# Expert stage: gate by tanh, rows stored already modulated, all low parts of the weights on VectorE

## The reference, cut to what matters

```python
x = x + ga1 * y                                   # y = hybrid_mixer(...)
h = rmsnorm(x, g_norm_ffn) * (1.0 + sc2) + sh2    # sh2, sc2, ga2 from silu(c) @ w_ada + b_ada
aff = softmax(h @ w_router)                       # 2048 x 16
g, idx = top_k(aff.T, 256)                        # per expert
xs = h[idx]                                       # 16 x 256 x 1024
a, u = xs @ w_gate, xs @ w_up                     # 16 x 256 x 768
out = rmsnorm(x + ga2 * scatter_add(idx, (silu(a) * u) @ w_down * g), g_final)
```

## Time and profile before

| what | value |
|---|---|
| median of 3 runs | 3539.58 us (3536.52 to 3541.98) |
| span of the profiled execution (its own time beyond the span isn't given) | 3526.4 us |
| PE, PEld busy | 3097.0 us (88%), 2192.4 us (62%) |
| DVE, ACT, POOL busy | 2266.7 (64%), 1427.3 (40%), 992.7 (28%) |
| mean granted TensorE clock | 0.934 |

### The profile page before, as it was taken

The page is one execution under the profiler, slowest core; times in us unless marked ns, Lnnn a source line. Parts: engine busy times, 40 slices in busy tenths (PEclk is TensorE's granted clock), DMA queues, the critical chain, the costliest instruction groups (busy, mean ns, idle before and its releaser), DMA issues. The chain is left out here.

```text
span 3526.4 us, 44830 instructions
## 1 busy us (share of the span) xinstructions
PE 3097.0 (88%) x14689; PEld 2192.4 (62%) x14689; DVE 2266.7 (64%) x2823; ACT 1427.3 (40%) x2136; POOL 992.7 (28%) x514
## 2 busy tenths in 40 slices
PE   6899999999786999999999988971988989899892
PEld 1455555555785556556555647850888878888782
DVE  1133333333675777777777764557888989889893
ACT  0133333332223566666556644330334343333433
POOL 0000001100453332332333212211445444444441
PEclk9999999999776999999999999985999999999996
DMA  8412111121322011011001004341565666656656
GB/s 320 149 59 69 59 59 64 66 67 48 102 89 58 4 31 31 5 31 31 23 13 29 5 20 157 125 141 57 156 203 169 191 186 181 196 165 195 190 145 226
DMA packets 252530, 362.92 MB, mean 103 GB/s; under 512 B 34356, under 2 KB 168503, under 8 KB 250808
## 3 DMA queue, kind: packets, MB, share of 16 engines
q1 hardware_dynamic: 243128, 326.91, 28.5%
q0 software_dynamic: 9216, 33.56, 4.3%
HBM read 278.60 MB, written 81.83 MB: 102 GB/s over the span
## 5 line engine op out<-in xcount | busy, mean ns | idle before, releaser
L465 PE MATMUL bank<-w_in_sb,h_T 128*128 128x512 f32 (+1 forms) x1440 | 610.2, 579 | 2.1 <-DVE h_T L614 2.1
L1614 PE MATMUL ebank<-gathered_T,w_gate_up 128*128 128x256 f32 x4608 | 564.9, 284 | 20.5 <-ACT w_gate_up L1656 12.7
L1614 PEld LDWEIGHTS ebank<-gathered_T,w_gate_up 128*128 128x128 f32 x4608 | 560.2, 190 | 24.4 <-issue 23.5
L1075 PE MATMUL abank<-scores,head_v 128*128 128x512 f32 x1152 | 546.0, 602 | 2.2 <-ACT scores L1113 2.2
L1038 PE MATMUL abank<-head_qT,head_kT 96*128 96x512 f32 x1728 | 504.6, 437 | 22.9 <-POOL head_qT L1017 22.9
L465 PEld LDWEIGHTS bank<-w_in_sb,h_T 128*128 128x128 f32 x1440 | 271.1, 191 | 298.9 <-issue 298.7
L1038 PEld LDWEIGHTS abank<-head_qT,head_kT 96*128 96x128 f32 x1728 | 327.7, 190 | 169.9 <-issue 94.7
L1024 POOL TENSOR_TENSOR scores<-scores,max_for_pool 128x1536 f32<-128x1536 f32 x64 | 221.1, 3476 | 570.9 <-ACT max_for_pool L1107 570.9
L1101 ACT ACTIVATE scores<-abank 128x512 f32<-128x512 f32 x576 | 314.2, 608 | 77.0 <-PE abank L1038 71.2
L1075 PEld LDWEIGHTS abank<-scores,head_v 128*128 128x128 f32 x1152 | 218.6, 194 | 180.3 <-issue 162.8
L1628 PE MATMUL ebank<-w_down,hidden_T 128*128 128x512 f32 x1152 | 303.0, 418 | 21.0 <-POOL w_down L1545 20.8
(11 more groups left out here) (261 smaller groups left out, 4138.3 us busy)
## 6 DMA issues: line engine op xcount, KB each, us to landing
w_gate_up_whole<-in_w_exp_gate SPq DMA_DIRECT2D x48, 1024.0 KB, 5.9
w_gate_up_whole<-in_w_exp_up SPq DMA_DIRECT2D x48, 1024.0 KB, 9.0
w_down_whole<-in_w_exp_down SPq DMA_DIRECT2D x192, 256.0 KB, 2.9
ada_w<-in_w_ada SPq DMA_DIRECT2D x12, 2048.0 KB, 12.8
scratch_ret<-ret_rows SPq DMA_DIRECT2D x72, 256.0 KB, 2.5
x_tile<-in_x_all SPq DMA_DIRECT2D x18, 512.0 KB
w_in_sb<-in_w_in SPq DMA_DIRECT2D x4, 2048.0 KB, 15.0
chunk_qk<-scratch_ret SPq DMA_DIRECT2D x16, 512.0 KB
```

Of the source, the lines that this page charges most:

```text
L465: m = pe.matmul(banks[bank][:, 0:n], hT[u][:, k, :], w_in[:, k, lo:lo + n], start=(k == 0), stop=(k == KD - 1))
L1075: m = pe.matmul(banks[5 + j % 2][:, :], v1[u][:, kt, :], sc[j % 2][:, kt, :], start=(kt == 0), stop=(kt == T - 1))
L1614: x = pe.matmul(banks[f % 3][:, j * CAP:(j + 1) * CAP], w_gu[c][:, wp, j, k, o:o + P], xsT[:, xp, k, :], start=(k == 0 and n == 0), stop=( ...
```

## The change

Four edits go together. (1) In mix_out the modulation is done on rows ahead of the transposes: x2 is multiplied by its statistic and the scale row, then the shift row is added, and the transposed halves are only copied from PSUM. The rows stored for the gather are so already modulated, and the expert stage has no modulate step; ACT rounds straight from the PSUM bank and DVE subtracts from it. (2) The two rows come from the columns: SP stores columns 24 to 39 to DRAM at the end of modulation, and mix_out loads them broadcast to all partitions. (3) The gate is x (1 + tanh(x / 2)) / 2. (4) DVE makes all low parts of the weights; POOL only issues its indirect DMAs.

```diff
@@ -226,6 +226,8 @@
+            sp.wait_ge(s_fold, 5)
+            sp.dma_start(scratch["ffn_rows"].rearrange("o (j p) -> p (o j)", p=P), perm["modcols"][:, 0, 24:40], allow_slow_non_contiguous=True).then_inc(perm["ffn_rows_stored"], 16)
@@ -1202,6 +1204,8 @@
+        xs = sb("x2_scaled", [P, D])
+        ffn_rows = sb("ffn_rows", [P, 2, D])
@@ -1241,6 +1245,8 @@
+            sp.wait_ge(perm["ffn_rows_stored"], 16)
+            sp.dma_start(ffn_rows[:, :, :].rearrange("p j d -> p (j d)"), scratch["ffn_rows"].partition_broadcast(P)).then_inc(r_loaded, 16)
@@ -1292,7 +1298,7 @@
             def router(m):
...
-                pe.wait_ge(r_loaded, 16)
+                pe.wait_ge(r_loaded, 32)
@@ -1353,12 +1359,9 @@
             def router(m):
...
-                    o = h2T[:, 4 * g:4 * g + 4, :]
...
-                    dve.tensor_tensor(o, banks[4 + g][:, :].rearrange("p (k n) -> p k n", k=4), last(perm["modcols"][:, 0, 32 + 4 * g:36 + 4 * g], P), ALU.mult).then_inc(sg["h2T"].sem, 1)
-                    sg["h2T"].wait(dve, m, 2 * g + 1)
-                    dve.tensor_tensor(o, o, last(perm["modcols"][:, 0, 24 + 4 * g:28 + 4 * g], P), ALU.add).then_inc(sg["h2T"].sem, 1)
+                    dve.tensor_copy(h2T[:, 4 * g:4 * g + 4, :].rearrange("p k n -> p (k n)"), banks[4 + g][:, :]).then_inc(sg["h2T"].sem, 1)
@@ -1389,7 +1392,12 @@
-                dve.tensor_scalar(xn[:, :], x2[u][:, :], st[:, 1:2], None, ALU.mult).then_inc(sg["x2_normed"].sem, 1)
+                if first:
+                    dve.wait_ge(r_loaded, 32)
+                dve.scalar_tensor_tensor(xs[:, :], x2[u][:, :], st[:, 1:2], ffn_rows[:, 1, :], ALU.mult, ALU.mult).then_inc(sg["x2_scaled"].sem, 1)
+                sg["x2_scaled"].wait(dve, m)
+                settled(dve)
+                dve.tensor_tensor(xn[:, :], xs[:, :], ffn_rows[:, 0, :], ALU.add).then_inc(sg["x2_normed"].sem, 1)
@@ -1535,24 +1542,9 @@
-            def rest_up(e, c):
-                sg["gu_rounded"].wait(pool, e, 2 * c + 2)
-                pool.tensor_tensor(w_gu[c][:, 1, 1], w_gu_whole[c][:, 1, 1], w_gu[c][:, 0, 1].bitcast(F32), ALU.subtract).then_inc(sg["up_rest"].sem, 1)
-            def rest_down(e, i):
-                sg["d_rounded"].wait(pool, e, i + 1)
-                x = w_d[i % RING]
-                pool.tensor_tensor(x[:, 1, :], w_d_whole[i % RING][:, 1, :], x[:, 0, :].bitcast(F32), ALU.subtract).then_inc(sg["d_rest_late"].sem, 1)
             def turn(e, u, ahead):
-                rest_up(e, 2)
...
-                    rest_up(e + 1, 0)
-                for i in range(RING, ND):
-                    rest_down(e, i)
-                if ahead:
-                    rest_up(e + 1, 1)
@@ -1594,7 +1584,7 @@
             def transposes(e, n):
...
-                sg["modulated"].wait(pe, e, 2 * (n - 2) + 1)
+                sg["gathered_rest"].wait(pe, e, n - 1)
@@ -1602,12 +1592,11 @@
             def gate_up(e, f):
...
-                sg["hidden"].wait(pe, e, 4 * (f - 2))
+                sg["hidden"].wait(pe, e, 2 * (f - 2))
...
-                sg["gate_rest"].wait(pe, e, c + 1)
-                sg["up_rest"].wait(pe, e, c + 1)
+                sg["gu_rest"].wait(pe, e, 2 * c + 2)
@@ -1620,7 +1609,7 @@
-                sg["d_rest"].wait(pe, e, i + 1) if i < RING else sg["d_rest_late"].wait(pe, e, i - RING + 1)
+                sg["d_rest"].wait(pe, e, i + 1)
@@ -1661,17 +1650,18 @@
             def round_gathered(e, n):
...
-                sg["modulated"].wait(act, e, 2 * n + 2)
-                act.activation(xsT[:, 0, 4 * g:4 * g + 4, h * P:(h + 1) * P], xm[n % 2][:, :, :], ACT.Copy).then_inc(sg["gathered_rounded"].sem, 1)
+                sg["xT_psum"].wait(act, e, n + 1)
+                sg["gu_psum"].wait(act, e - 1)
+                act.activation(xsT[:, 0, 4 * g:4 * g + 4, h * P:(h + 1) * P], banks[6 + n % 2][:, :].rearrange("p (k n) -> p k n", k=4), ACT.Copy).then_inc(sg["gathered_rounded"].sem, 1)
...
             def round_hidden(e, f):
-                sg["hidden"].wait(act, e, 4 * f + 4)
+                sg["hidden"].wait(act, e, 2 * f + 2)
...
             def gate_exp(e, f):
...
-                act.activation(ex[f % 2][:, :], banks[f % 3][:, 0:CAP], ACT.Exp, scale=-1.0).then_inc(sg["gate_exp"].sem, 1)
+                act.activation(ex[f % 2][:, :], banks[f % 3][:, 0:CAP], ACT.Tanh, scale=0.5).then_inc(sg["gate_exp"].sem, 1)
@@ -1808,26 +1798,16 @@
-            def modulate(e, n):
-                h, g = n // 2, n % 2
-                x = xm[n % 2][:, :, :]
-                sg["gu_psum"].wait(dve, e - 1)
-                sg["gathered_rest"].wait(dve, e, n - 1)
-                sg["xT_psum"].wait(dve, e, n + 1)
-                dve.tensor_tensor(x, banks[6 + n % 2][:, :].rearrange("p (k n) -> p k n", k=4), last(perm["modcols"][:, 0, 32 + 4 * g:36 + 4 * g], P), ALU.mult).then_inc(sg["modulated"].sem, 1)
-                sg["modulated"].wait(dve, e, 2 * n + 1)
-                dve.tensor_tensor(x, x, last(perm["modcols"][:, 0, 24 + 4 * g:28 + 4 * g], P), ALU.add).then_inc(sg["modulated"].sem, 1)
             def rest_gathered(e, n):
...
-                dve.tensor_tensor(xsT[:, 1, o[0], o[1]], xm[n % 2][:, :, :], xsT[:, 0, o[0], o[1]].bitcast(F32), ALU.subtract).then_inc(sg["gathered_rest"].sem, 1)
-            def rest_gate(e, c):
-                sg["gu_rounded"].wait(dve, e, 2 * c + 1)
-                dve.tensor_tensor(w_gu[c][:, 1, 0], w_gu_whole[c][:, 1, 0], w_gu[c][:, 0, 0].bitcast(F32), ALU.subtract).then_inc(sg["gate_rest"].sem, 1)
+                dve.tensor_tensor(xsT[:, 1, o[0], o[1]], banks[6 + n % 2][:, :].rearrange("p (k n) -> p k n", k=4), xsT[:, 0, o[0], o[1]].bitcast(F32), ALU.subtract).then_inc(sg["gathered_rest"].sem, 1)
+            def rest_gate_up(e, c):
+                for j in range(2):
+                    sg["gu_rounded"].wait(dve, e, 2 * c + j + 1)
+                    dve.tensor_tensor(w_gu[c][:, 1, j], w_gu_whole[c][:, 1, j], w_gu[c][:, 0, j].bitcast(F32), ALU.subtract).then_inc(sg["gu_rest"].sem, 1)
@@ -1838,14 +1818,10 @@
-                dve.tensor_scalar(x[:, :], x[:, :], 1.0, None, ALU.add).then_inc(s.sem, 1)
-                s.wait(dve, e, 4 * f + 1)
-                dve.reciprocal(x[:, :], x[:, :]).then_inc(s.sem, 1)
-                s.wait(dve, e, 4 * f + 2)
-                dve.tensor_tensor(x[:, :], banks[f % 3][:, 0:CAP], x[:, :], ALU.mult).then_inc(s.sem, 1)
-                s.wait(dve, e, 4 * f + 3)
+                dve.scalar_tensor_tensor(x[:, :], x[:, :], 1.0, banks[f % 3][:, 0:CAP], ALU.add, ALU.mult).then_inc(s.sem, 1)
+                s.wait(dve, e, 2 * f + 1)
...
-                dve.tensor_tensor(x[:, :], banks[f % 3][:, CAP:], x[:, :], ALU.mult).then_inc(s.sem, 1)
+                dve.scalar_tensor_tensor(x[:, :], x[:, :], 0.5, banks[f % 3][:, CAP:], ALU.mult, ALU.mult).then_inc(s.sem, 1)
@@ -1858,18 +1834,11 @@
-            def gathered(e):
-                for n in range(4):
-                    modulate(e, n)
-                    if n:
-                        rest_gathered(e, n - 1)
-                rest_gathered(e, 3)
             def turn(e, u, ahead):
...
-                rest_gate(e, 2)
+                rest_gate_up(e, 2)
@@ -1883,40 +1852,40 @@
-                    rest_gate(e + 1, 0)
+                    rest_gate_up(e + 1, 0)
...
-                    modulate(e + 1, 0)
+                    rest_gathered(e + 1, 0)
...
+                for i, n in ((6, 1), (7, 2), (8, 3)):
+                    rest_down(e, i)
+                    if ahead:
+                        rest_gathered(e + 1, n)
+                for i in range(9, ND):
+                    rest_down(e, i)
+                for n in range(4):
+                    y_rows(e, u, n)
...
-                    for n in range(1, 4):
-                        modulate(e + 1, n)
-                        rest_gathered(e + 1, n - 1)
-                    rest_gathered(e + 1, 3)
-                y_rows(e, u, 0)
-                y_rows(e, u, 1)
-                y_rows(e, u, 2)
-                y_rows(e, u, 3)
-                if ahead:
-                    rest_gate(e + 1, 1)
+                    rest_gate_up(e + 1, 1)
...
-                rest_gate(0, c)
-            gathered(0)
+                rest_gate_up(0, c)
+            for n in range(4):
+                rest_gathered(0, n)
...
-                "slots_psum": 1, "xT_psum": 4, "modulated": 8, "gate_exp": 6, "hidden": 24}
-EXPERT_STEPS_AGAIN = {"gu_rounded": ("x_rstd", 6), "gate_rest": ("x_normed", 3), "up_rest": ("xT_psum", 3),
-                      "d_rounded": ("hT", 12), "d_rest": ("z_psum", 6), "d_rest_late": ("z_latent", 6),
+                "slots_psum": 1, "xT_psum": 4, "gate_exp": 6, "hidden": 12}
+EXPERT_STEPS_AGAIN = {"gu_rounded": ("x_rstd", 6), "gu_rest": ("xT_psum", 6),
+                      "d_rounded": ("hT", 12), "d_rest": ("z_psum", 12),
```

(1 more changed line is left out.)

10 lines of the change are left out of this document (5 added, 5 removed).

## The result

The changed kernel takes 3555.63 us (median of five runs, 3553.79 to 3565.92) against 3539.60 (3536.52 to 3541.98) before: a ratio of 1.0044, 95% interval 1.0033 to 1.0056, so 16 us slower. The two profiled spans differ by more, 3556.1 against 3526.4.

| stage, us | before | after | difference | forecast |
|---|---|---|---|---|
| start of mixer output (holds the late first x tile) | 2123.90 | 2132.64 | +8.7 | +3.5 |
| mixer output | 234.1 | 282.2 | +48.1 | +31 |
| from there to the first gate-up (search, first gather) | 114.2 | 103.7 | -10.5 | -4 |
| 15 expert turns | 937.8 | 921.5 | -16.3 | -6 |
| last turn and tail | 116.4 | 116.0 | -0.4 | 0 |

What follows compares the result with a forecast made beforehand. The prediction took TensorE to set the time in the projection, mixer output and expert turns. It summed +31 + 3.5 - 6 - 4 = +24.5 on the 3526.4 span, plus 13.2 around it, to 3564 us, range 3538 to 3592.

Steps and rivals of the forecast that it cites:

- Part 1, ring: Mixer output: two row operations lengthen the dependency cycle through DVE and the transposes by 1.8 us a tile, 27 over 15.
- Part 1, clock: Mixer output: TensorE's 2.0 us rest per tile lowers its clock at times; +4 us over 16 tiles, bounds 0 and 25.
- count of three in eight: Expert stage: three in eight TensorE waits of 1.9 to 2.8 us were followed by low clock, each costing 1.7 us.
- mixer clock: Rival, mixer output: a 2.0 us rest drops the clock in every tile, the ring grows by 1.7 more; 3585 us, chance 0.12.
- Part 2, store: Projection start: storing 16 columns as separate 4-byte words delays the x tile queued behind; +3.5 us, bounds 0 and 12.
- price per piece: Columns' store: 41 ns per piece on each of 16 engines, from measured stores; 128 pieces per engine take 5.3 us.
- Part 3, the wait: Expert turn: the fourth transposes wait 4.3 us for bank 7, behind ACT's round of the late seventh down slice; clock falls.
- T: Expert turn: the end of gate-up, from which later steps are timed; transposes 3 were forecast to start at T + 11.4.
- Part 3, the loop gaps: Expert turns: six gaps of about 2.5 us where a loop iteration begins were kept as 1.1 us per turn.
- turns near 61 and 63.5 alternating: Sign that the forecast is right: expert turns take about 61 and 63.5 us by turns.
- Part 4: Start of expert stage: copy and rest per group replace four operations, first gate-up at 2468.4 instead of 2472.2; -4 us.
- Sum: Whole kernel: +31 + 3.5 - 6 - 4 = +24.5 on the span of 3526.4, plus 13.2 to the median: 3564 us.

Runs made afterwards that it cites:

- e6: Changed kernel with eight more unread 128x512 matmuls per mixer-output tile, between the first half and the transposes: 3565.9 us, ratio 1.0044 to 1.0093 against before.
- e3: Changed kernel with the three later rounds of gathered rows ahead of w_down's seventh slice on ScalarE, low parts likewise on VectorE: 3474.6 us.
- e11: Changed kernel with forty small unread matmuls (128x16) added once, in TensorE's pause ahead of the first slots: 3592.3 us, ratio 1.0124 to 1.0158 against before.
- e9: Kernel before with all low parts of the weights on VectorE, reciprocals and modulation kept: 3537.4 us, ratio 0.9967 to 0.9996.
- e12: Kernel before with only the store of the 16 columns added, ahead of the first x tile, read by nothing: 3551.3 us, ratio 1.0004 to 1.0042.
- e1: Changed kernel with plain rows to the transposes again and stored rows modulated in their own buffer after the transposes' release: 3529.6 us.
- e7: Changed kernel with stored rows modulated in VectorE's pause before the next tile's normalisation, columns' store behind x tiles, gathered-row rounds first: 3414.0 us.

## Why the prediction was right, and where not

The side and the shape were right: two losses ahead of the expert stage, a wait there that only changes its cause. That the total came within 8 us was in good part luck: one term was short by 17, another by 5, and two gains of 10 and 7 were not foreseen. By steps:

- **Part 1, ring.** 1.8 us a tile forecast, 1.9 measured (e6: period 15.95, forecast 15.8). The two operations take 1.29 and 1.23, and between them stand 0.15 us, not 0.05.
- **Part 1, clock.** "I take +4 for 16 tiles, bounds 0 and 25": it was 19.3. The count of three in eight, at 1.7 us each over 15 tiles, would itself have given 9.6, so the +4 did not follow from it. It was made over single waits in the expert stage; here a wait of 2.1 us comes in every tile, and 11 of 16 second halves ran slow (6.5 to 7.8 us). The rival *mixer clock* came true for the most part, at its own condition ("if the rest passes some 2 us"). This is the largest mis-sized term.
- **Part 2, store.** +3.5 forecast, 9 us in the traces, inside its bounds of 0 and 12. Its own terms, 5.3 less 1.4, make 3.9. The mis-sized term is the price per piece: 128 words on each of 16 engines at 41 ns gave 5.3 us; to come 9 us late behind a start 1.3 us earlier, the store held the queue for about 10.3, an average of 80 ns a word. The mechanism was another than a price per packet: all words had passed by 123.5, 2.7 us after the store's issue, and the wait was for its landing, 12.0 us after the issue. The Trainium skill ("DMA: Bandwidth & Descriptors", Bandwidth) gave an estimate of 21.5 for the whole store; the measured 10.3 lie between the two.
- **Part 3, the wait.** Right in place, cause and size: T + 11.5 and 4.24 to 4.52 us in 14 of 15 turns (5.67 in the last), with the low clock behind it; e3 shows it by removing it. The turn of 62.0 was 61.4. (15 of 62.0 and 2.1 are 932.1, not 931.5.)
- **Part 3, the loop gaps.** "1.1 (six loop gaps over 15)" kept: this step failed. Summed they fell from 15.0 to 4.1 us, which is as much as the 10 us by which the turns came out below the forecast, and the sign "turns near 61 and 63.5 alternating" did not come: they are 60.2 to 62.6 throughout. e6 and e11 show that such pauses come and go with the place of the loop; that the change itself moved it into a better place is likely from that and was not isolated.
- **Part 4.** -4 forecast, -3.7 measured (20.91 to 17.26 from the slots' matmuls to the first gate-up). The search's -6.8 was not seen: I looked at POOL's first subtractions as work given to DVE, not as a collision with DVE's search; e9 shows it alone.
- **Sum.** On the spans +24.5 was forecast and +29.7 measured, two mis-sized losses (+17 and +5) against two unforeseen gains (-10 and -7). "13.2 above it, which I take as what lies around" was wrong: every run has 2 us around its span. The profiled execution of before was a quick one, at 3526.4 + 2 below the runs timed beside the changed kernel (3536.5 and up); it has the short value of the untouched stages, and turns of 937.8 where e12 has 943.3. So 3564 less 11, plus the 5.2 that the sum was short of, is 3558.3, the profiled run; the median lies 2.7 below it. The two errors partly cancelled, which was luck too.

So was the change sound? Tanh was the gain (57 us in the turns). The low parts on DVE without a new order gave 41 of it back, and all of it (57) if the loop pauses are left out. The rows cost 48 + 9 and gave 4 at the stage's start, and next to nothing in the turns (4 without the loop pauses) until the order was mended (33.6 then).

## What to carry to other kernels

When an operation moves to an engine that works through a list, ask what its place in the list waits for: three rounds behind a late load cost 55 to 88 us here, an edit of two lines. Work that is added to an engine with idle time should go where the idle time is, not next to the data: the same two row operations cost 48, 11 or 0 us in three places. And compare stages between traces, not totals: three effects of 8 to 23 us here (a store ahead of a load, the place of a loop, two levels of untouched stages) hide in a total that moved by 16.

## What the runs showed of the hardware

- Forty matmuls that cost nothing themselves made 15 later loop turns 23 us slower (e11); pauses behind the loop's branch are 0 to 1.3 us in one position and up to 4.6 (1.22 and 3.42 together) in another.
- With a rest of 2.1 us in every tile of 17 the granted clock of a stretch was 0.91; with 1.98 us of filler in it the clock was 1.00, and the stage ended 19.3 us sooner although TensorE did more (e6). With waits of only 0.4 to 0.6 us it was 0.95 (e1).
- 2048 words of 4 bytes to DRAM delayed the load queued behind them by 9 us: their packets had passed within 2.7 us of the issue, the store landed after 12.0, and until then the queue moved 29 GB/s instead of 391.
- A two-input operation of 128x48 on VectorE took 4.06 us instead of 0.21 when GpSimd had started a subtraction of 4.54 us just before it (before).
- Two dependent 128x1024 operations on VectorE, with the wait that joins them, left 0.15 us between them (e1, e7).
